# SyncE issues the chunk of the 128-slot stream before the chunk of the 64-slot stream in a two-layer hybrid mixer with experts

## The chip, the cores and the metric

The kernel is one program on one NeuronCore of a Trainium2 chip. TensorE (PE) multiplies, VectorE (DVE) and ScalarE (ACT) work elementwise, GpSimd (POOL) sets up constants, SyncE (SP) issues the transfers. They run side by side and meet through semaphores. Sixteen DMA engines bring weights from HBM into SBUF. The metric is the device time of one launch in microseconds, median of the runs; lower is better.

## The reference

Two layers work on 256 latent tokens and 256 context tokens of width 1024. Each layer is a modulated RMSNorm, an input projection, a mixer of three head groups, an output projection, then a second norm and a channel mixer. The channel mixer of the second layer is the part that matters here: eight SwiGLU experts of hidden width 2816, of which each token takes the best two.

```python
def swiglu(h, w1, w3, w2):
    return (jax.nn.silu(h @ w1) * (h @ w3)) @ w2

def moe_swiglu(h, w_r, b_r, w1, w3, w2):
    logits = (h @ w_r).astype(jnp.float32) + b_r.astype(jnp.float32)
    top_v, top_i = lax.top_k(logits, TOP_K)
    probs = jax.nn.softmax(top_v, axis=-1)
    combine = jnp.einsum('blk,blke->ble', probs, jax.nn.one_hot(top_i, N_EXPERTS, dtype=jnp.float32))
    out = jnp.zeros_like(h)
    for e in range(N_EXPERTS):
        out = out + combine[..., e, None].astype(h.dtype) * swiglu(h, w1[e], w3[e], w2[e])
    return out
```

All weights are float32. The three matrices of one expert are 34.6 MB, so the stage reads 277 MB.

## The kernel before

The first half of the program holds both mixers and the dense channel mixer of layer 0. The expert stage starts at about 820 us of the profiled span and ends at about 1582. It alone is touched.

Tokens are gathered into slots by expert. The experts are ordered by load. The four fuller ones form the t stream, with 128 slots each; the four emptier ones form the s stream, with 64 slots each. The fullest expert has 32 more slots, the x stream, which uses the t stream's weights in the first pass. A pass (`pair` on SyncE, `expert` on the other engines) works on one t expert and one s expert together; there are four passes.

The weights of an expert are cut into 33 chunks of 1 MiB (`PER_EXPERT`): 22 of w1 and w3 (`UP`), 11 of w2. Most are 128x2x1024, rows of 4 KB; chunks 16, 17, 19, 20 are 128x4x512 and chunks 18 and 21 are 128x8x256. In step j of a pass TensorE does the following:

- the t matmuls of chunk j (L1218 on), in three products of a high and a low part. ScalarE writes the high part `w_hi` from `raw` (L1589), VectorE the low part `w_lo` (L2187). There are three buffers for each part, so the split of chunk j+3 waits for TensorE's t matmuls of chunk j and for the landing of chunk j+3;
- the s matmuls of chunk j (`s_mm`), in full float32 and straight from the landed tile. They wait for the landing alone and end with an increment of `s_pe`;
- in the first pass, the x matmuls of chunk j+3, also straight from the t stream's landed tile.

Landed tiles: `raw` has five slots. Slots 0 to 2 are the ring of the t stream; slots 3 and 4 and the tile `raw_x` are the ring of the s stream. So every third s chunk goes through `raw_x`, which makes it easy to follow in the trace.

All these transfers are issued by SyncE, in program order, on one queue. SyncE itself waits until a slot is free. A slot of the t stream is free once VectorE has written `w_lo` from it (function `taken`, a wait on `dve_done`) and, in the first pass, once the x matmuls have used it. A slot of the s stream is free after the s matmuls (wait on `s_pe`). In step j of `pair` the s chunk that is issued is j+3 (`RING`), the t chunk is j+6 (`RING + AHEAD`). The first pass is written out, the second and third run in a hardware loop, the fourth is written out with `last=True` and stops issuing when there is nothing left to fetch.

Of the kernel before, what the change touches and what calls it, by code (L numbers as in the profile page):

```python
# [64 lines left out]
PER_EXPERT = UP + DOWN  # L65
# [9 lines left out]
RING = 3  # L75
# [126 lines left out]
def program(nc, a, out, known, marks):  # L202
    def at(*name):

        return known[name] if known else 1

    ctx = ExitStack()
    with ctx:
        def sem(name):
            return ctx.enter_context(nc.semaphore(name))  # L210
# [160 lines left out]
        s_dve, s_act, s_pe = sem("s_dve"), sem("s_act"), sem("s_pe")  # L371
# [97 lines left out]
        def s_raw(j):  # L469
            return raw_x[:, :] if j % RING == RING - 1 else raw[:, RING + j % RING, :]  # L470
# [21 lines left out]
        def _(sp):  # L492
# [42 lines left out]
            def expert_chunk(e, j, slot, landed):  # L535

                if j < UP:
                    m, k0, nk, c0, nc_ = UPC[j]
                    src = a[("moe_w1", "moe_w3")[m]][0].rearrange("e (k p) c -> (e k) p c", p=P)
                    src = src[bass.ds(e * KD + k0, nk), :, c0:c0 + nc_]  # L540
                    sp.dma_start(slot.rearrange("p (k c) -> p k c", k=nk), src.rearrange("k p c -> p k c"))\
                      .then_inc(landed[E_SLOT[j]], 16)
                else:
                    src = a["moe_w2"][0].rearrange("e (k p) c -> (e k) p c", p=P)
                    src = src[bass.ds(e * KF + 2 * (j - UP), 2), :, :]
                    sp.dma_start(slot.rearrange("p (k c) -> p k c", k=2), src.rearrange("k p c -> p k c"))\
                      .then_inc(landed[E_SLOT[j]], 16)

            K = at("per_expert", "dve")
            last = {E_SLOT[j]: j for j in range(PER_EXPERT)}  # L550

            def taken(j, shift):
                if j < PER_EXPERT:
                    sp.wait_ge(dve_done, (at("first_lo", j) if shift is None else at("e_lo", j) + shift) if j >= SPL or
                               shift is None else at("next_lo", j) - K + shift)
                else:
                    sp.wait_ge(dve_done, at("next_lo", j - PER_EXPERT) + shift)

            def t_chunk(e, j):
                expert_chunk(e, j, raw[:, E_SLOT[j], :], exp_in)  # L560

            def s_chunk(e, j):
                expert_chunk(e, j, s_raw(j), s_in)

            def pair(e, e_s, after, after_s, n, top=False, last=False):
                for j in range(PER_EXPERT):
                    if not last or j + RING < PER_EXPERT:
                        sp.wait_ge(s_pe, at("s_mm", j) + n * Ks)
                        s_chunk(e_s if j + RING < PER_EXPERT else after_s, (j + RING) % PER_EXPERT)
                    t = j + RING + AHEAD  # L570
                    if not last or t < PER_EXPERT + RING:
                        taken(j + AHEAD, n * K)
                        if top and j + AHEAD < PER_EXPERT:
                            sp.wait_ge(x_pe, at("x_mm", j + AHEAD))
                        t_chunk(e if t < PER_EXPERT else after, t % PER_EXPERT)

            def expert_of(turn):
                return sp.value_load(order_i[0:1, bass.ds(turn, 1)], min_val=0, max_val=NE - 1)
# [11 lines left out]
            Ks = at("per_s", "pe")  # L590
# [4 lines left out]
            e_s = expert_of(NE)  # L595
            for j in range(RING):
                s_chunk(e_s, j)
            for j in range(AHEAD):
                taken(j, None)
                sp.wait_ge(x_pe, at("x_mm", j))  # L600
                t_chunk(e, j + RING)
            pair(e, e_s, expert_of(1), expert_of(NE + 1), 0, top=True)
            with sp.Fori(1, NT - 1, 1) as n:
                pair(expert_of(n), expert_of(n + NE), expert_of(n + 1), expert_of(n + NE + 1), n)
            sp.wait_ge(x_dve, at("again"))
            pair(expert_of(NT - 1), expert_of(TURNS - 1), expert_of(NT), None, NT - 1, last=True)

            with sp.Fori(0, MORE, 1) as r:
# [116 lines left out]
        def _(pe):  # L725
# [10 lines left out]
            def tables(n):  # L736

                _, rows, _ = TABLES[n]
                return nc.tensor.transpose(STAT[:, P * n:P * n + rows], rows_sb[0:rows, n, :], ident[0:rows, 0:rows])
# [92 lines left out]
            def first_products(l):  # L832

                pe.wait_ge(dve_done, at("h_lo", l, 1, 0))
                take(("w_in", l, WIN_ORDER[0]))
                for k in range(KD):
                    pe.wait_ge(dve_done, at("h_lo", l, 1, k))
                    product(l, 0, 0, k)
                    if l == 1 and k == 0:
                        take(("w_in", l, WIN_ORDER[1]))  # L840
                    if l == 0 and k == 1:
                        product(l, 0, 1, k)
                        take(("w_in", l, WIN_ORDER[1]))
                        product(l, 1, 0, 0)
                        product(l, 1, 0, 1)
                    elif l == 1 or k > 1:
                        product(l, 1, 0, k)
                        product(l, 0, 1, k)
                    else:
                        product(l, 0, 1, k)  # L850
                    if l == 1:
                        product(l, 1, 1, k)
                if l == 0:
                    pe.wait_ge(table_in, 16 * sum(len(parts) for parts, _, _ in TABLES[1:]))
                    pe.wait_ge(dve_done, at("t", 0, 1, KD - 1))
                    for m in range(1, len(TABLES)):
                        i = tables(m)
                    i.then_inc(pe_done, pe_n("tables"))
                    for k in range(KD):
                        product(l, 1, 1, k)  # L860
# [244 lines left out]
            def turn_bank_free(j, de, ae, sd, sa, top, s):  # L1105

                users = [(SEL_AT, "sel", 0)] + [(at_, "t", p) for p, at_ in TURN_AT.items()]
                users += [(S_SEL_AT, "s_sel", 0)] * s + [(at_, "s", g) for g, at_ in S_TURN_AT.items() if s]
                users += [(X_SEL_AT, "x_sel", 0)] * top + [(at_, "x", n) for n, at_ in X_TURN_AT.items() if top]
                assert len({u[0] for u in users}) == len(users)  # L1110
                _, kind, n = max(u for u in users if u[0] < j)
                if kind == "sel":
                    pe.wait_ge(act_done, at("e_selT") + ae)
                    pe.wait_ge(dve_done, at("e_slot_w") + de)
                elif kind == "t":
                    pe.wait_ge(dve_done, at("e_hd", n) + de)
                elif kind == "s_sel":
                    pe.wait_ge(s_dve, at("s_selT") + sd)
                elif kind == "s":
                    pe.wait_ge(s_act, at("s_hd", n) + sa)  # L1120
                elif kind == "x_sel":
                    pe.wait_ge(x_dve, at("x_selT"))
                else:
                    pe.wait_ge(x_act, at("x_hd", n))
# [1323 lines left out]
```

## Time and profile before

| | |
|---|---|
| median of 3 runs | 1620.76 us (1618.61 to 1623.23) |
| profiled execution | 1618.61 us |
| its span | 1616.8 us |
| mean granted TensorE clock | 0.968 |
| busy PE / DVE / ACT | 1508.7 / 845.7 / 622.7 us |
| read from HBM | 395.55 MB |
| transfers of expert weights | 223 to `raw`, 44 to `raw_x`, 1 MiB each, median 8.4 and 8.3 us from issue to landing |

The profile is one execution of the program. The span runs from its first instruction to its last; the execution's time is 1.8 us longer. Of the other runs it differs by what one run differs from the next. "Busy" is time in which an engine executes; SyncE isn't counted, since it only issues and waits. In the rows below L541 and L546 are SyncE's issues of w1 or w3 and of w2 chunks, L727 is the helper through which every matmul goes, and the names before and behind the arrow are the written and the read tiles. s matmuls read `raw` or `raw_x` with `hcs` (gathered tokens) in the w1 and w3 part and with `xT` (where the hidden activations stand by then) in the w2 part; x matmuls read `raw` with `hcx`. An "idle before" in brackets names what ended it.

### The profile page before, as it was taken

How to read it: one execution, taken by the hardware profiler on the slowest of the kernel's cores; microseconds unless marked ns; L12 is line 12 of the kernel's file. 1: busy time of each engine (PE TensorE's matmuls, PEld its weight loads, DVE VectorE, ACT ScalarE, POOL GpSimd, SP SyncE). 2: the span in 40 equal slices, each digit the busy share in tenths (PEclk: the TensorE clock that was granted, in tenths of full speed). 3: DMA queues.
4: the chain of work that ended last, by engine and by line, in shares of the span. 5: the costliest groups of instructions: out<-in, count | busy, mean ns of one | idle time of the engine just before them, and what ended most of it. 6: DMA issues, size and time to landing. Idle time of an engine off the chain costs nothing.

```text
span 1616.8 us, 22394 instructions
## 1 busy us (share of the span) xinstructions
PE 1508.7 (93%) x8914; PEld 1063.4 (66%) x8915; DVE 845.7 (52%) x1115; ACT 622.7 (39%) x679; POOL 17.4 (1%) x56
## 2 busy tenths in 40 slices
PE   5999798999999998976879999999999999999995
PEld 3786485888888876953745575665766566655763
DVE  2898845333333234897564544445554555355544
ACT  2426723222123223457253433434443444344441
POOL 2000000000000001000000000000000000000000
PEclk9999899999999999997989999999999999999996
DMA  9632943822442233436269999889999999999990
GB/s 335 204 104 85 337 127 140 212 72 72 131 119 73 72 114 105 157 104 243 72 263 355 344 325 353 306 326 399 389 409 377 396 382 408 386 350 396 393 388 28
DMA packets 208664, 398.10 MB, mean 246 GB/s; under 512 B 12060, under 2 KB 123056, under 8 KB 208560
## 3 DMA queue, kind: packets, MB, share of 16 engines
q1 hardware_dynamic: 207968, 396.42, 68.4%
q8 instruction: 76, 1.25, 0.3%
q10 hardware_dynamic: 592, 0.21, 0.1%
q14 instruction: 28, 0.23, 0.0%
HBM read 395.55 MB, written 1.05 MB: 245 GB/s over the span
## 4 chain that ended last, share of the span: by engine, by line
PE 83%; DVE 6%; ACT 5%; DMA 3%; issue 3%; DVEq 0%; SPq 0%; ACTq 0%
PE bank L727 81%; DMA raw<-in_w_mod 2%; DVE xc L1986 1%; PE bank L1201 1%; DVE y L1884 1%; DVE tb L1756 1%; DVE h_lo L1764 1%; ACT la L1476 1%; DMA raw<-in_moe_w 1%; ACT w_hi L1355 0%; ACT li L1472 0%; ACT lr L1470 0%; ACT w_hi L1589 0%; ACT lm L1481 0%; DVE w_lo L1739 0%
## 5 line engine op out<-in xcount | busy, mean ns | idle before, releaser
L2187 DVE TENSOR_TENSOR w_lo<-raw,w_hi 128x2048 fp32r<-128x2048 f32 x135 | 309.3, 2292 | 268.4 <-ACT w_hi L1589 261.0
L1589 ACT ACTIVATE w_hi<-raw 128x2048 fp32r<-128x2048 f32 x135 | 258.2, 1913 | 429.0 <-PE bank L727 318.0
L727 PE MATMUL bank<-h_hi,w_hi 128*128 128x512 f32 (+1 forms) x768 | 285.7, 372 | 18.7 <-DVE h_lo L1764 16.3
L727 PE MATMUL bank<-h_lo,w_hi 128*128 128x512 f32 (+1 forms) x768 | 283.0, 369 | 0.0
L727 PE MATMUL bank<-h_hi,w_lo 128*128 128x512 f32 (+1 forms) x768 | 282.8, 368 | 0.0
L1355 ACT ACTIVATE w_hi<-raw 128x2048 fp32r<-128x2048 f32 (+1 forms) x64 | 113.7, 1776 | 214.6 <-PE bank L727 196.7
L727 PEld LDWEIGHTS bank<-h_hi,w_hi 128*128 128x128 f32 x768 | 147.1, 192 | 46.5 <-DVE h_lo L1764 19.8
L1739 DVE TENSOR_TENSOR w_lo<-raw,w_hi 128x2048 fp32r<-128x2048 f32 (+1 forms) x64 | 135.9, 2123 | 51.2 <-ACT w_hi L1355 51.0
L727 PEld LDWEIGHTS bank<-h_hi,w_lo 128*128 128x128 f32 x768 | 146.9, 191 | 23.5
L727 PEld LDWEIGHTS bank<-h_lo,w_hi 128*128 128x128 f32 x768 | 147.1, 191 | 23.0
L727 PE MATMUL bank<-w_hi,hc_hi 128*128 128x512 f32 (+1 forms) x384 | 153.8, 400 | 1.9 <-ACT w_hi L1589 1.9
L727 PE MATMUL bank<-w_lo,hc_hi 128*128 128x512 f32 (+1 forms) x384 | 144.6, 376 | 0.0
L727 PE MATMUL bank<-w_hi,hc_lo 128*128 128x512 f32 (+1 forms) x384 | 143.8, 374 | 0.0
L727 PE MATMUL bank<-raw,hcs 128*64 128x512 f32 (+2 forms) x736 | 116.5, 452 | 0.0
L727 PEld LDWEIGHTS bank<-w_hi,hc_hi 128*128 128x128 f32 x384 | 72.6, 189 | 47.0 <-issue 23.9
L727 PEld LDWEIGHTS bank<-w_hi,hc_lo 128*128 128x128 f32 x384 | 72.7, 189 | 14.3
L727 PEld LDWEIGHTS bank<-w_lo,hc_hi 128*128 128x128 f32 x384 | 72.9, 190 | 10.4
L2090 DVE TENSOR_TENSOR sq<-tb,bank 128x512 f32<-128x512 f32 x22 | 15.1, 688 | 121.0 <-ACT tb L1555 121.0
L727 PEld LDWEIGHTS bank<-raw,hcs 128*64 128x64 f32 x736 | 43.6, 136 | 48.1 <-issue 42.5
L727 PE MATMUL bank<-w_hi,hd_hi 128*128 128x512 f32 x176 | 73.0, 415 | 0.0
L1555 ACT ACTIVATE tb<-bank 128x512 f32<-128x512 f32 x22 | 13.2, 598 | 153.6 <-PE bank L727 153.6
L727 PE MATMUL bank<-f_hi,w_hi 128*128 128x512 f32 x176 | 69.1, 393 | 0.0
(299 smaller groups left out, 1862.7 us busy)
## 6 DMA issues: line engine op xcount, KB each, us to landing
raw<-in_moe_w SPq DMA_DIRECT2D x223, 1024.0 KB, 8.4
raw<-in_w_mod SPq DMA_DIRECT2D x48, 1024.0 KB, 7.8
raw_x<-in_moe_w SPq DMA_DIRECT2D x44, 1024.0 KB, 8.3
raw<-in_ffn_w SPq DMA_DIRECT2D x44, 512.0 KB, 5.4
raw<-in_w_in SPq DMA_DIRECT2D x18, 1024.0 KB, 5.3
raw<-in_ffn_w SPq DMA_DIRECT2D x16, 704.0 KB, 4.7
raw<-in_w_out SPq DMA_DIRECT2D x8, 1024.0 KB, 5.5
x_in<-in_ctx SPq DMA_DIRECT2D x1, 1024.0 KB, 4.9
```

Of the source, the lines that this page charges most:

```text
L727: return nc.tensor.matmul(dst, lhsT, rhs, start=first, stop=last)
L1201: i = nc.tensor.transpose(bank[TURN_BANK][:, P * t:P * t + P], hid[:, p % 2, P * t:P * t + P], ident[:, :])
L1355: nc.scalar.activation(w_hi[:, s % SPL, 0:n], raw[:, POS[c] % RAW, 0:n], ACT.Copy)\
L1476: nc.scalar.activation(la[:, t, :], lr[:, t, :], ACT.Exp, scale=cln[:, k:k + 1], bias=cln[:, k:k + 1]).then_inc(act_done, act_n())
L1589: nc.scalar.activation(w_hi[:, j % SPL, :], raw[:, E_SLOT[j], :], ACT.Copy)\
L1739: V.tensor_tensor(w_lo[:, s % SPL, 0:n], raw[:, POS[SPLIT[s]] % RAW, 0:n], w_hi[:, s % SPL, 0:n].bitcast(F32), ALU.subtract).then_inc(dve_ ...
L1756: i = V.scalar_tensor_tensor(tb[:, d % 2, tok(s)], xT[:, d, tok(s)], amp[:, l, w - 1, d, s:s + 1], STAT[:, tok(s)], ALU.mult, ALU.mult)
L1764: i = V.scalar_tensor_tensor(h_lo[:, d, tok(s)], tb[:, d % 2, tok(s)], shift, h_hi[:, d, tok(s)].bitcast(F32), ALU.add, ALU.subtract)
L1884: i = V.scalar_tensor_tensor(out_v, in_v, w, out_v, ALU.mult, ALU.add)
L1986: i = V.scalar_tensor_tensor(out_v, cxp[:, t, :, k:k + 256], w, out_v, ALU.mult, ALU.add)
L2090: V.tensor_tensor(sq[:, i11 % 2, :], tb[:, i11 % 2, :], bank[2 * (s0 % 3) + 1][:, :], ALU.mult)\
L2187: V.tensor_tensor(w_lo[:, j % SPL, :], raw[:, E_SLOT[j], :], w_hi[:, j % SPL, :].bitcast(F32), ALU.subtract).then_inc(dve_done, dve_n(name ...
```

## The change

In each step of `pair` the two blocks are exchanged. Before, SyncE waited for the s matmuls of step j and issued the s chunk, then waited for the split and issued the t chunk. Now the t chunk's waits and issue come first. The transfers, their sizes, their slots and the conditions of each are the same; only SyncE's order differs. The order of the instructions on the four other engines is unchanged.

```diff
             def pair(e, e_s, after, after_s, n, top=False, last=False):
                 for j in range(PER_EXPERT):
-                    if not last or j + RING < PER_EXPERT:
-                        sp.wait_ge(s_pe, at("s_mm", j) + n * Ks)
-                        s_chunk(e_s if j + RING < PER_EXPERT else after_s, (j + RING) % PER_EXPERT)
                     t = j + RING + AHEAD
                     if not last or t < PER_EXPERT + RING:
                         taken(j + AHEAD, n * K)
                         if top and j + AHEAD < PER_EXPERT:
                             sp.wait_ge(x_pe, at("x_mm", j + AHEAD))
                         t_chunk(e if t < PER_EXPERT else after, t % PER_EXPERT)
+                    if not last or j + RING < PER_EXPERT:
+                        sp.wait_ge(s_pe, at("s_mm", j) + n * Ks)
+                        s_chunk(e_s if j + RING < PER_EXPERT else after_s, (j + RING) % PER_EXPERT)
```

SyncE at the start of the hardware loop over the second and third pass, steps 0 to 2, before. An ISA row with a wait is a wait that stands by itself; s_pe counts the s matmuls, dve_done VectorE's instructions.

```order
L568 ISA
L541 ISA [waits s_pe]
L541 DMA raw_64<-in_moe_w1 128x2x1024
L554 ISA
L541 ISA [waits dve_done]
L541 DMA raw_64<-in_moe_w3 128x2x1024
L568 REGISTER_ALU
L541 ISA [waits s_pe]
L541 DMA raw_64<-in_moe_w3 128x2x1024
L554 REGISTER_ALU
L541 ISA [waits dve_done]
L541 DMA raw_64<-in_moe_w3 128x2x1024
```

The same place in the changed kernel.

```order
L554 ISA
L541 ISA [waits dve_done]
L541 DMA raw_64<-in_moe_w3 128x2x1024
L574 ISA
L541 ISA [waits s_pe]
L541 DMA raw_64<-in_moe_w1 128x2x1024
L554 REGISTER_ALU
L541 ISA [waits dve_done]
L541 DMA raw_64<-in_moe_w3 128x2x1024
L574 REGISTER_ALU
L541 ISA [waits s_pe]
L541 DMA raw_64<-in_moe_w3 128x2x1024
```

The s chunk 3 (w1, behind the wait on s_pe) stood in front of the t chunk 6 (w3, behind the wait on dve_done); now it stands behind it, and so in each step.

The same exchange further on in the loop, where the t stream fetches chunks 16 and 17 (128x4x512) and the s stream chunks 13 and 14, before.

```order
L554 REGISTER_ALU
L541 ISA [waits dve_done]
L541 DMA raw_64<-in_moe_w1 128x4x512
L568 REGISTER_ALU
L541 DMA raw_x_68<-in_moe_w3 128x2x1024 [waits s_pe]
L554 REGISTER_ALU
L541 ISA [waits dve_done]
L541 DMA raw_64<-in_moe_w1 128x4x512
```

And in the changed kernel.

```order
L541 ISA [waits dve_done]
L541 DMA raw_64<-in_moe_w1 128x4x512
L574 REGISTER_ALU
L541 DMA raw_64<-in_moe_w3 128x2x1024 [waits s_pe]
L554 REGISTER_ALU
L541 ISA [waits dve_done]
L541 DMA raw_64<-in_moe_w1 128x4x512
L574 REGISTER_ALU
L541 DMA raw_x_68<-in_moe_w3 128x2x1024 [waits s_pe]
```

Between the two t chunks there stood the s chunk for `raw_x` (chunk 14); now chunk 13 stands there and the chunk for `raw_x` comes behind the second t chunk.

## Rows read from the trace of the kernel before

**Rows 1.** The page: busy time of each engine over the span.

```profile
PE 1508.7 (93%) x8914; PEld 1063.4 (66%) x8915; DVE 845.7 (52%) x1115; ACT 622.7 (39%) x679; POOL 17.4 (1%) x56
```

**Rows 2.** Busy time by stretch, one expert pass (us, busy and count, clock, DMA share, GB/s).

```profile
1212.00:1390.00 178.00, 177.79 (x915) 111.49 (x915) 93.58 (x73) 75.46 (x61) 0.00 (x0) 1.00 1.02 393
```

**Rows 3.** Waits, 1028 to 1582 us (who for whom: us in total, times, longest).

```profile
ACT w_hi L1589 <- DMA raw<-in_moe_w: 104.0, 35, 4.1
PEld bank L727 <- DMA raw_x<-in_moe_w: 1.4, 4, 0.4
```

**Rows 4.** Instructions in order of time near 1239 us (start, length, engine, operation).

```profile
1236.97 1.94 PE L727 MATMUL bank<-raw,hcs 128*64 128x512 f32 x8
...
1239.09 0.37 SPq L541 DMA_DIRECT2D raw<-in_moe_w  x1
...
1239.10 2.29 DVE L2187 TENSOR_TENSOR w_lo<-raw,w_hi 128x2048 fp32r<-128x2048 f32 x1 [1.06 <-ACT w_hi L1589]
...
1241.57 0.37 SPq L541 DMA_DIRECT2D raw<-in_moe_w  x1
```

**Rows 5.** The tile raw, the one transfer issued at 1241.57 us.

```profile
DMA to landing us min/median/max: 5.1/5.1/5.1
```

**Rows 6.** DMA throughput in 40 slices, 1228 to 1268 us, then 1268 to 1388 us.

```profile
GB/s 414 385 426 377 262 311 410 418 422 410 98 0 119 373 414 393 422 414 418 410 422 422 401 406 426 410 401 401 418 410 401 393 414 356 414 381 307 406 365 258
...
GB/s 391 397 416 408 414 411 408 397 396 395 402 356 380 391 384 377 350 357 400 395 402 363 396 411 407 411 410 410 408 406 412 407 411 408 412 407 408 408 407 411
```

**Rows 7.** Busy tenths of the DMA engines in 40 slices, 1048 to 1088 us.

```profile
DMA  8999699993000007899999999999989999999999
```

**Rows 8.** ScalarE and weight loads near 1347 us; the tile raw_x, 1330 to 1350 us.

```profile
1344.42 1.92 ACT L1589 ACTIVATE w_hi<-raw 128x2048 fp32r<-128x2048 f32 x1 [3.25 <-DMA raw<-in_moe_w]
1349.55 1.92 ACT L1589 ACTIVATE w_hi<-raw 128x2048 fp32r<-128x2048 f32 x1 [2.72 <-DMA raw<-in_moe_w]
...
1347.30 0.20 PEld L727 LDWEIGHTS bank<-raw_x,xT 128*64 128x64 f32 x4 [0.36 <-DMA raw_x<-in_moe_w]
...
L546 SPq DMA_DIRECT2D raw_x<-in_moe_w x2: 372/372/373, 1334.4 to 1349.5; - x2
DMA to landing us min/median/max: 12.5/12.6/12.8
```

**Rows 9.** The tile raw_x and the matmuls that use the transfer, one pass earlier, one later.

```profile
L546 SPq DMA_DIRECT2D raw_x<-in_moe_w x1: 372/372/372, 1172.6 to 1172.6; - x1
DMA to landing us min/median/max: 12.5/12.5/12.5
...
1185.57 0.65 PE L727 MATMUL bank<-raw_x,xT 128*64 128x512 f32 x2
...
L546 SPq DMA_DIRECT2D raw_x<-in_moe_w x1: 372/372/372, 1515.0 to 1515.0; - x1
DMA to landing us min/median/max: 12.6/12.6/12.6
...
1527.86 0.65 PE L727 MATMUL bank<-raw_x,xT 128*64 128x512 f32 x2
```

**Rows 10.** The t stream near 1345 us: the split of a chunk, and its first matmul.

```profile
1341.21 2.29 DVE L2187 TENSOR_TENSOR w_lo<-raw,w_hi 128x2048 fp32r<-128x2048 f32 x1 [2.27 <-ACT w_hi L1589]
...
1349.59 0.48 PE L727 MATMUL bank<-w_hi,hd_hi 128*128 128x512 f32 x1
```

**Rows 11.** The tile raw_x in the first pass, 860 to 1030 us.

```profile
DMA to landing us min/median/max: 4.8/5.0/8.3
```

**Rows 12.** TensorE's short idle in the first pass; busy time and clock there and after 1403.

```profile
898.24 1.07 PE L727 MATMUL bank<-raw,hcx 128*32 128x256 f32 x16 [0.58 <-ACT gsx L1606]
...
890.00:900.00 10.00, 9.42 (x70) 5.06 (x67) 6.23 (x8) 3.83 (x4) 0.00 (x0) 1.00 0.93 330
...
1402.84 0.49 PE L727 MATMUL bank<-w_hi,hc_hi 128*128 128x512 f32 x1 [1.86 <-ACT w_hi L1589]
...
1403.00:1407.00 4.00, 4.00 (x11) 3.13 (x12) 1.67 (x2) 0.00 (x0) 0.00 (x0) 0.57 1.01 387
```

## The prediction

> **What bounds the kernel now.** I read the page's busy line first: TensorE is busy 93% of the span, more than any other engine [rows 1]. The change touches only SyncE's issue order in the expert stage, so I then read the stretches by expert pass. In the third pass TensorE is busy 177.79 of 178 us at clock 1.00, while the DMA engines are busy too (share 1.02, 393 GB/s) [rows 2]. Both are full at once, so what counts is who waits for whom. Over the last three passes ScalarE waits for weights 35 times, 104.0 us in all, but the array's weight loads wait for a landing in raw_x only 4 times, 1.4 us together [rows 3], and those short waits lie under matmuls that still run. TensorE sets the time, and transfers arrive just before they are needed.
>
> The two streams of weights have very different reserves. I read them at chosen chunks, as landing against first use.
>
> The s stream (64 slots, matmuls straight from the landed tile): the chunk issued at 1334.4 lands 12.5 us later, at 1346.9, and its first weight load starts at 1347.30, released by that landing [rows 8]. Reserve 0.4 us. One pass earlier: 1172.6 + 12.5 = 1185.1 against 1185.57, reserve 0.5. One pass later: 1515.0 + 12.6 = 1527.6 against 1527.86, reserve 0.3 [rows 9].
>
> The t stream (128 slots, split by ScalarE and VectorE first): the chunk whose split ends on VectorE at 1341.21 + 2.29 = 1343.50 meets its first matmul at 1349.59 [rows 10]. Reserve 6.1 us.
>
> **How the transfers run.** A t chunk lands at 1344.42 (ScalarE starts on it at once) and the next at 1349.55; an s chunk lands between them, at 1346.9 [rows 8]. They alternate as SyncE's list does, one chunk per 5.13 / 2 = 2.56 us, or 1.049 MB / 2.56 us = 409 GB/s, which the slices show (407 to 412) [rows 6]. With 12.5 us from issue to landing, four to five chunks stand ahead of a new one. So in this stretch the moment of issue matters little, the place in the row decides. By the Trainium skill, "DMA: Bandwidth & Descriptors", section Queues, rings and completion order, completion is not in order per issuing engine: a later transfer may finish first. The rows above show landings in order of issue; if the rule held here, the first rival's sum (+6.2 us) would apply.
>
> The row is not always full. After each change of pass the transfers catch up and the engines run dry: 98, 0 and 119 GB/s in the three slices from 1238 to 1241 [rows 6], zeros near 1060, one pass earlier [rows 7]. From 1241 to 1388 no slice is empty. Whatever the new order loses at the dry spot stays lost for the rest of the pass.
>
> **The change, part by part.** It removes and adds no instruction. In each of the 33 steps of a pass, SyncE now first waits for VectorE's split of t chunk j+3 and issues t chunk j+6, and only then looks at TensorE's s matmuls of step j and issues s chunk j+3.
>
> 1. The wait in front of the s chunk. At the dry spot the s matmuls of the step run 1236.97 to 1238.91, and the s chunk is issued at 1239.09. The split ends at 1239.10 + 2.29 = 1241.39, and the t chunk is issued at 1241.57 [rows 4]. In the new order the s chunk can't go before that: 1241.57 - 1239.09 = 2.48 us later.
> 2. The chunk ahead of it. The t chunk now finds the row empty; the s chunk starts when it is through, 2.56 us on. Together 2.48 + 2.56 = 5.04 us later than before.
> 3. The t chunk gains nothing. It starts at 1241.57 in either order: it was behind an s chunk that started at 1239.09 and was through at 1241.65, and it lands 5.1 us after issue [rows 5]. Its reserve was 6.1 us anyway, so an earlier landing shortens only ScalarE's wait, which nobody waits for. That excludes a gain from this side.
> 4. From there the row is full, t and s alternate, and every s chunk lands about 5.04 us later against an unmoved TensorE. Where the reserve was 0.4 us, TensorE must be late by 5.04 - 0.4. Nothing pays it back: TensorE is busy 99.9% of the pass [rows 2], so its delay goes to the end.
> 5. The waits queued behind. SyncE does nothing else in this stage. The t chunk behind a late s chunk has its 6 us of reserve plus TensorE's own delay. ScalarE and VectorE keep their order.
> 6. The first pass: s chunks take 4.8 to 8.3 us there [rows 11]. From issue to use are at least the 12.9 us of the later pass (1334.4 to 1347.3) plus three blocks of a third stream's matmuls, 1.07 us each [rows 12], 16.1 us. The reserve is 7.8 us or more, over 5.04. No cost. It is the same at each change of pass, where the transfers have caught up. So three passes pay.
>
> Sum: 3 x 5.04 - (0.5 + 0.4 + 0.3) = 13.9 us. The profiled execution took 1618.61 us (span 1616.8), so 1632.5 in its terms. The median of the runs shown is 1620.76, 2.15 us above it, which gives 1634.7. I forecast 1634.5 us.
>
> Bounds of the shift per pass, since no row shows SyncE in the new order: at least 2.48 us (the wait alone counts), 3 x 2.48 - 1.2 = +6.2 us; at most a whole split in front of the s chunk, 1.92 us on ScalarE [rows 8] and 2.29 us on VectorE [rows 10], if TensorE's s matmuls are through before it begins: 4.21 + 2.56 = 6.77 us per pass, 3 x 6.77 - 1.2 = +19.1. I take 5.04, since the rows of the dry spot are the place where it is decided.
>
> A chunk's price could be seen otherwise. The same page of the Trainium skill, section Bandwidth (Where 436 GB/s comes from), says that HBM binds at about 358 GB/s for one core. A chunk would then take 1.049 / 358 = 2.93 us, and the sum would be 1.1 us higher. The slices here hold 407 to 412 GB/s, so the measurement decides against it.
>
> **Rivals.**
>
> *Only one of the two terms counts.* If landings were not strictly in order of issue, or the row had slack later, the shift would be the wait alone: +6.2 us, 1626.9 by the median. For it: the order is read from few chunks. Against it: no empty slice after 1241, and steady 2.56 us steps.
>
> *The waits also lower the clock.* TensorE will now stand still often for some tenths of a us. After an idle of 1.86 us before 1402.84 the clock was 0.57 of full over 1403 to 1407 [rows 12], which costs 4 x 0.43 = 1.7 us. Against it: idle of 0.58 us at 897.7 stands beside a clock of 1.00 from 890 to 900 [rows 12]. One such fall per pass gives 13.9 + 5.1 = +19.0, 1639.8; two give 1644.9.
>
> *Not slower.* The reserve at the tight point is what is left after a long catch-up race. From 1246.67 (1241.57 + 5.1) to 1344.42 there are 36 chunks, 2.71 us each, not 2.56: slices of 350 to 391 GB/s from 1301 to 1325 [rows 6], where the chunks come in smaller pieces. If the new order let all run at 2.56 us, 36 x 0.15 = 5.5 us per pass would come back, more than the loss. It decides once 3 of these 5.5 us come back: +13.9 - 9.0 = +4.9, which is 0.3%; with all of it 13.9 - 16.5, 1618 or so. Against it: pieces and sizes are unchanged. I give it an even result of about 1624.
>
> **How the numbers follow.** Forecast 0.62 (its own range 1631 to 1638), one term only 0.16, clock 0.14, not slower 0.08. The range 1626 to 1641 leaves out most of the last and about half of the clock's cases. A difference under 0.3% (4.9 us) can't be told from none with this kernel. Slower by over 0.3%: 0.62 + 0.14 and three quarters of 0.16, 0.88. Within: 0.04 from the one-term case and 0.06, 0.10. Faster: 0.02.
>
> **What the new profile would show.**
> - SyncE's issues in pairs, t chunk first, s chunk within about 0.5 us behind it. If the s chunk comes 2 us later still, step 1 is too small.
> - Slices of the DMA engines as full as before from the dry spot on. If there are new empty slices, step 4 is wrong upwards.
> - TensorE idle before matmuls on raw and raw_x, released by their landing: some 14 us in all, from about step 13 to 26 of the last three passes, none over 1 us, none in the first pass. If it is near 6 us, the one-term case holds; if near zero, the mechanism is wrong.
> - The raw_x flight in the tight stretch shorter, 10.5 to 11 us, not 12.5: issued with the t chunk, yet landing three steps of 5.13 us after the one before.
> - ScalarE's 104.0 us of waiting for landings falls under 20 us, because TensorE becomes the later of its two conditions.
> - Clock 1.00 in the passes but for one stretch near 1405.
>
> The forecast is wrong if s chunks keep landing where they did, or if the clock falls at the new waits.

## The result, and the profile after

The changed kernel takes 1634.73 us (median of 5 runs, 1630.55 to 1637.11); the kernel before takes 1620.76 (median of 5 on the same chip, 1616.17 to 1623.74). The ratio is 1.0085, 95% interval 1.0059 to 1.0110: slower by 14.0 us, where 13.9 was worked out and 1634.5 forecast. The profiled execution took 1638.21 us (span 1636.5), somewhat above the median.

The page of the changed kernel, busy time first and then the chain of waits:

```profile
PE 1514.5 (93%) x8914; PEld 1068.2 (65%) x8915; DVE 846.9 (52%) x1115; ACT 622.5 (38%) x679; POOL 17.4 (1%) x56
...
PE 70%; DMA 11%; DVE 9%; ACT 6%; issue 3%; SPq 1%; DVEq 0%; ACTq 0%
PE bank L727 68%; DMA raw<-in_moe_w 5%; DMA raw_x<-in_moe_w 4%; DVE w_lo L2187 2%; ACT w_hi L1589 2%; DMA raw<-in_w_mod 2%; DVE y L1884 1%; DVE xc L1986 1%; DVE tb L1756 1%; ACT la L1476 1%; DVE w_lo L1739 1%; DVE h_lo L1764 1%; DVE lr L2033 1%; ACT li L1472 0%; ACT lr L1470 0%
```

Every engine does the same instructions as in [rows 1]. What is new stands in the chain: transfers of expert weights into raw and raw_x hold 9% of it. Before, the chain was 83% TensorE and 3% DMA.

The four expert passes of the changed kernel as stretches, columns as in [rows 2]:

```profile
836.80:1045.20 208.40, 205.81 (x1473) 124.84 (x1465) 93.64 (x107) 75.04 (x66) 0.00 (x0) 0.99 0.91 331
1045.20:1232.50 187.30, 182.41 (x925) 115.22 (x921) 93.07 (x73) 75.31 (x62) 0.00 (x0) 0.99 0.97 370
1232.50:1417.40 184.90, 179.68 (x909) 112.26 (x905) 93.52 (x74) 75.82 (x62) 0.00 (x0) 0.99 0.99 376
1417.40:1601.20 183.80, 179.14 (x907) 112.09 (x905) 93.06 (x73) 75.38 (x62) 0.00 (x0) 0.99 0.95 365
```

The same four passes of the kernel before:

```profile
836.80:1043.20 206.40, 204.15 (x1469) 123.59 (x1461) 93.13 (x107) 75.07 (x66) 0.00 (x0) 1.00 0.93 338
1043.20:1223.50 180.30, 180.30 (x923) 113.63 (x921) 92.84 (x73) 75.37 (x62) 0.00 (x0) 1.00 1.00 382
1223.50:1402.50 179.00, 177.27 (x907) 110.56 (x905) 93.61 (x75) 77.39 (x63) 0.00 (x0) 1.00 1.02 392
1402.50:1581.60 179.10, 178.46 (x905) 111.71 (x905) 92.02 (x72) 73.89 (x61) 0.00 (x0) 0.99 0.96 368
```

Length less busy time is TensorE's idle time. In the last three passes it is 4.89 + 5.22 + 4.66 = 14.8 us after, and 0 + 1.73 + 0.64 = 2.4 us before. With 0.3 us in the first pass (2.59 against 2.25) that makes 12.7 of the 19.6 us between the two sums. The rest is busy time: 5.2 us in the last three passes and 1.7 in the first, most of it clock (four falls against one, below). The DMA share falls only because the same transfers now stand in a longer time.

The waits of the changed kernel, 1028 to 1600 us, which answer to [rows 3]:

```profile
ACT w_hi L1589 <- PE bank L727: 329.4, 98, 11.7
...
PEld bank L727 <- DMA raw<-in_moe_w: 16.5, 25, 1.6
...
PE bank L727 <- DMA raw<-in_moe_w: 11.4, 17, 1.4
...
PEld bank L727 <- DMA raw_x<-in_moe_w: 10.0, 18, 1.2
...
PE bank L727 <- DMA raw_x<-in_moe_w: 2.1, 4, 0.8
```

The matmuls themselves now wait for a landing 21 times, 13.5 us together, where [rows 3] had only weight loads that waited for it. ScalarE's 104.0 us of waiting for landings are gone: TensorE is always the later of its two conditions.

The dry spot of the same pass as in [rows 4], in order of time:

```profile
1246.02 1.94 PE L727 MATMUL bank<-raw,hcs 128*64 128x512 f32 x8
...
1248.15 2.29 DVE L2187 TENSOR_TENSOR w_lo<-raw,w_hi 128x2048 fp32r<-128x2048 f32 x1 [1.06 <-ACT w_hi L1589]
...
1250.62 1.00 SPq L541 DMA_DIRECT2D raw<-in_moe_w  x2
...
1251.24 0.37 SPq L541 DMA_DIRECT2D raw<-in_moe_w  x1
```

The s matmuls are through at 1247.96, the split at 1250.44, and SyncE then issues two chunks in a row, at 1250.62 and 1251.24 (the first issue row holds both, the last one is the second of them by itself). The s chunk goes 1251.24 - 1247.96 = 3.28 us after its matmuls, where it was 0.18 us before. The tile raw, the transfers issued at 1250.62 (t) and at 1251.24 (s), which answer to [rows 5]:

```profile
DMA to landing us min/median/max: 5.5/5.5/5.5
...
DMA to landing us min/median/max: 7.4/7.4/7.4
```

The t chunk finds the row empty; the s chunk lands at 1258.6, 2.5 us behind it. DMA throughput in 40 slices, 1232 to 1272 us, which answers to [rows 6]:

```profile
GB/s 168 422 422 418 426 238 205 385 434 414 406 377 410 381 401 426 258 49 4 66 188 401 422 422 414 389 369 418 401 401 340 319 393 385 410 389 307 426 426 389
```

Here and below, "the row" is the line of chunks that are issued and not yet landed. It runs dry at 1248 and is back by about 1252.5 (the slice of 1252 is 46% full), 19.6 us after the pass's first t matmul at 1232.9. In [rows 6] it is back by about 1240.7 (119 of 410 GB/s in that slice), 16.9 us after that pass's first t matmul at 1223.8: 2.7 us earlier. After it no slice is empty, as before.

Two of the new waits, in the same pass (TensorE in order of time):

```profile
1335.02 1.20 PE L727 MATMUL bank<-raw,hcs 128*64 128x128 f32 x18 [1.00 <-DMA raw<-in_moe_w]
...
1351.98 0.44 PE L727 MATMUL bank<-raw,hcs 128*64 128x128 f32 x4 [1.36 <-DMA raw<-in_moe_w]
```

And the tile raw_x between them, issued at 1350.8, against 12.5 us in [rows 8]:

```profile
L546 SPq DMA_DIRECT2D raw_x<-in_moe_w x1: 373/373/373, 1350.8 to 1350.8; - x1
...
DMA to landing us min/median/max: 11.3/11.3/11.3
```

### The profile page after: what moved, and what is told of

It reads as the page before. It is cut to its first block, busy times and chain, and to the rows that moved or that the text cites. A ratio compares the mean times of both kernels' runs of the same rounds, so it can differ in the third digit from the quotient of the medians.

```text
span 1636.5 us, 22394 instructions
## 1 busy us (share of the span) xinstructions
PE 1514.5 (93%) x8914; PEld 1068.2 (65%) x8915; DVE 846.9 (52%) x1115; ACT 622.5 (38%) x679; POOL 17.4 (1%) x56
## 4 chain that ended last, share of the span: by engine, by line
PE 70%; DMA 11%; DVE 9%; ACT 6%; issue 3%; SPq 1%; DVEq 0%; ACTq 0%
PE bank L727 68%; DMA raw<-in_moe_w 5%; DMA raw_x<-in_moe_w 4%; DVE w_lo L2187 2%; ACT w_hi L1589 2%; DMA raw<-in_w_mod 2%; DVE y L1884 1%; DVE xc L1986 1%; DVE tb L1756 1%; ACT la L1476 1%; DVE w_lo L1739 1%; DVE h_lo L1764 1%; DVE lr L2033 1%; ACT li L1472 0%; ACT lr L1470 0%
## 5 line engine op out<-in xcount | busy, mean ns | idle before, releaser
L727 PEld LDWEIGHTS bank<-h_hi,w_lo 128*128 128x128 f32 x768 | 146.2, 190 | 23.7
L727 PE MATMUL bank<-raw,hcs 128*64 128x512 f32 (+2 forms) x736 | 116.5, 452 | 10.7 <-DMA raw<-in_moe_w 10.5
L2090 DVE TENSOR_TENSOR sq<-tb,bank 128x512 f32<-128x512 f32 x22 | 15.1, 688 | 121.4 <-ACT tb L1555 121.4
L727 PE MATMUL bank<-w_lo,hd_hi 128*128 128x512 f32 x176 | 71.2, 404 | 0.0
```

Source lines behind the costliest of these rows:

```text
L727: return nc.tensor.matmul(dst, lhsT, rhs, start=first, stop=last)
L2090: V.tensor_tensor(sq[:, i11 % 2, :], tb[:, i11 % 2, :], bank[2 * (s0 % 3) + 1][:, :], ALU.mult)\
```

## The experiments

All times are medians, and each ratio is against the kernel before on the same chip (1621.82 for the first four, 1621.54 for the next four, 1622.24 for the last two). "Waits for landings" are the rows PE bank <- DMA of the expert passes, as above. "Shift" is how much later an s chunk lands against the first t matmul of its pass than in the first profile of the kernel before. Every run on record has a mean granted clock; a span times (1 less that clock) is an estimate of what the lower clock cost it, about 53 us in the kernel before, nearly all of it outside the expert passes. The code cuts are shortened.

**The new order in the first pass alone.** Theory: the first pass has reserve and pays nothing.

```
for give in (give_t, give_s) if top else (give_s, give_t):   # each the old lines
    give()
```

> The new order in the first pass only; the other three passes as before. Theory (an s chunk lands 2.48 + 2.56 us later, and only passes whose reserve falls to 0.3 to 0.5 us pay): the first pass has 7.8 us of reserve or more, so TensorE waits for no s chunk and the time is that of before, within 0.3%; no idle of TensorE released by a landing after 860 us. Rival (the swap costs wherever it stands, about a quarter of +14 us per pass): +3.5 us, and waits of TensorE in the first pass.

Measured: 1623.29 us, ratio 1.0007 (0.9984 to 1.0030). Waits of this kernel, 1028 to 1610 us:

```profile
PEld bank L731 <- DMA raw_x<-in_moe_w: 2.5, 7, 0.4
...
PE bank L731 <- DMA raw<-in_moe_w: 0.2, 1, 0.2
```

No cost, as expected: the one idle of 0.2 us lies in the fourth pass, which has the old order. The first pass is safe in either order.

**The new order in steps 0 to 9 of each pass alone.** The dry spot lies in them.

```
for give in (give_t, give_s) if j < 10 else (give_s, give_t):
    give()
```

> The new order in steps 0 to 9 of every pass, the order of before from step 10 on. This keeps the loss at the dry spot and gives the s chunk its place in the row back before the tight stretch. Theory: s chunks land 2.48 us late in the tight stretch, TensorE idles 3 x 2.48 - 1.2 = 6.2 us by landings, time +6 us. Rival A (the dry spot does not matter, the order in the tight stretch does): idle 0, time as before. Rival B (everything is lost at the dry spot): idle near 14 us, as in the changed kernel.

Measured: 1634.16 us, ratio 1.0062 (1.0038 to 1.0086). TensorE's waits for landings in this kernel:

```profile
PE bank L731 <- DMA raw<-in_moe_w: 3.3, 6, 0.8
...
PE bank L731 <- DMA raw_x<-in_moe_w: 0.2, 1, 0.2
```

The shift of s chunk 12 is about 5 us (72.1 against 66.7 us after the start of the second pass); at chunk 13, the first with s first again, it falls by 2.5 to 2.6 us in each pass, and 2 to 3 us stay (4.2 late in the second pass). So the place in the row comes back when the order is turned back, and the part lost at the dry spot does not.

The sizes were missed: 3.5 us of waits for landings where 6.2 were expected, and 12.3 us of time (by the ratio 10.1) where 6 were. A good part of the excess is clock. In the profile the five stretches of half clock cost about 11.5 us, against 1.7 in the kernel before, and TensorE's idle in the last three passes is 9.9 us against 2.4; together 17 of the 18.9 us between the two spans. Over the runs on record the mean clock is 0.9648 in nine of this kernel and 0.9673 in 26 of the kernel before: by the estimate above about 4 us more, which leaves some 7 of the 11.6 us between the mean spans. Why the clock is lower here stays open.

**The new order from step 10 on alone.** The theory of the prediction expects the place alone, 2.56 us per pass.

```
for give in (give_t, give_s) if j >= 10 else (give_s, give_t):
    give()
```

> The other half: the order of before in steps 0 to 9 of every pass, the new order from step 10 on. Theory: only the chunk in front counts, 2.56 us and at most 0.4 us more where the row isn't quite full at step 10: TensorE idles 3 x 2.56 - 1.2 = 6.5 us up to 7.7 us by landings, time +7 us. Rival A: near 14 us, as in the changed kernel. Rival B: idle near 0, time as before.

Measured: 1631.18 us, ratio 1.0054 (1.0033 to 1.0075). Waits of this kernel, 1028 to 1610 us:

```profile
PE bank L731 <- DMA raw<-in_moe_w: 8.1, 13, 1.4
PE bank L731 <- DMA raw_x<-in_moe_w: 4.3, 3, 2.0
```

The expectation was missed: 12.4 us of idle, well over the 6.5 to 7.7. The kernel's transfers where the order changes, 1285 to 1305 us in 40 slices:

```profile
GB/s 410 410 410 426 401 410 393 418 410 410 410 410 418 410 393 352 205 139 123 307 365 418 373 393 430 418 418 401 361 250 332 385 377 406 397 410 414 422 403 315
```

The kernel before over the same time (its pass began 5.6 us earlier):

```profile
GB/s 393 426 410 401 410 401 401 426 410 418 385 389 393 389 393 393 393 401 393 401 401 418 373 393 389 397 393 410 410 406 416 377 369 360 354 350 348 354 373 383
```

The row was not full: it falls to 123 GB/s at 1294. In the steps around it a chunk's flight is 8.0 to 8.7 us, 3.0 to 3.7 over the 5.0 of a chunk alone, so a little over one chunk (2.56 us) stands ahead. An issue that comes 3 us later uses that up, and the landings pause. At s chunk 13, the first behind the turn, the shift jumps by 3.1 to 3.6 us: the place, and 0.5 to 1.0 of pause. By s chunk 18 it is near 5 us again (5.1, 5.6 and 3.8 in the three passes). So "unfilled time" adds to "place in the row" where the row is shallow, not at the dry spot only.

That does not explain all of the 5 us. In the third and fourth pass s chunk 17 lands 4.2 us behind the chunk in front of it, where the kernel before has 2.7 (in the third pass it is issued at 1313.0 and flies 12.2 us, the chunk in front 1312.4 and 8.6), and TensorE's longest idle of this kernel, 1.9 and 2.0 us, is the wait for it. The row is deep there and no slice from 1316 to 1332 is under 335 GB/s. What holds this chunk back stays open.

**The new order from step 20 on.** If the row's depth decides, there it is over two chunks (flights of 11.4 to 12.0 us in the third pass) and must hide the later issue, leaving the place alone.

```
for give in (give_t, give_s) if j >= 20 else (give_s, give_t):
    give()
```

> The order of before in steps 0 to 19 of every pass, the new order from step 20 on. With the swap from step 10 on TensorE had waited for s landings nearly as long as in the changed kernel (about 15 us, not the 6.5 to 7.7 that I had expected), and the first t chunk after the swap landed 6.2 us after its issue: the row was little over one chunk deep there, so an s chunk that comes 3 us late leaves a pause. Theory now: the shift is the place (2.56 us) plus what the later issue leaves unfilled, and at step 20 an s chunk takes 10.8 to 11.7 us to land in the kernel before, over two chunks stand ahead, so nothing stays unfilled: shift 2.56 us, waits for s landings 3 x 2.56 - 1.2 = 6.5 us. Rival (a swap costs two chunks' time wherever it stands, whatever the depth): 13 us or more.

Measured: 1628.23 us, ratio 1.0041 (1.0026 to 1.0056). Transfers at the turn, 1328 to 1348 us, and the waits of this kernel:

```profile
GB/s 387 406 393 393 410 422 406 385 389 393 385 397 393 414 397 414 401 375 387 391 334 342 354 383 391 385 410 393 401 410 393 426 418 410 418 401 401 410 393 434
...
PEld bank L731 <- DMA raw_x<-in_moe_w: 8.1, 5, 2.7
PE bank L731 <- DMA raw_x<-in_moe_w: 5.8, 3, 2.2
```

No hole. The landings after the turn stay 2.5 to 2.7 us apart, and the s chunks are late by one place, once per pass: from s chunk 22 to 23 the shift jumps by 2.5 to 2.6 us, and the longest wait at the weight loads is 2.7. TensorE's idle is 5.8 us where 6.5 were expected, the time 6.0 us more than before. So the place by itself is shown, with its size; the other term is what the dry spot and the turn at step 10 add to it.

**Is it the row at all, or SyncE's order and its waits?** The changed order, but each t chunk loads only its first 0.5 MiB. Half of the t weights are not loaded, so part of the computation is left out.

```
 sp.dma_start(raw[:, E_SLOT[j], 0:CW // 2]..., src[first half])   # 0.5 MiB, same waits, new order
```

> The changed order, but each t chunk loads only its first half, 0.5 MiB (the second half of the slot keeps old values, so that part of the computation is changed). A pair then takes 3.8 us of transfer and not 5.1, and TensorE needs about 5 us for a step. Theory: the row is never full, the s reserve never shrinks below about 3 us, TensorE does not wait although SyncE has exactly the order and the waits of the changed kernel: time as before, 1616 to 1624 us. Rival (SyncE's added wait costs by itself): still +6 us or more over before.

Measured: 1621.02 us, ratio 0.9995 (0.9977 to 1.0012). Of waits for landings, this one row is left:

```profile
PEld bank L736 <- DMA raw_x<-in_moe_w: 0.4, 1, 0.4
```

That is the weight loads; no matmul waits for a landing. The same instructions, waits and order cost nothing once the row has room. What costs is the full row. Two things lie under the equal time: the mean clock was lower (0.9646 against 0.9677, about 5 us by the estimate), and none of the idles that the kernel before has in its last three passes (2.4 us) is left in the list of waits. No run has the light row in the old order, so the argument rests on the waits more than on the time.

**The t chunk in two halves, the s chunk between them; and both halves behind it as a control.** The s chunk then has half a chunk ahead of it.

```
t_half(..., 0)      # waits for the split, as t_chunk did; 0.5 MiB
s_chunk(...)        # waits for the s matmuls
t_half(..., 1)      # the control: s_chunk first, then both halves
```

> Each t chunk is fetched in two transfers of 0.5 MiB; SyncE waits for the split, issues the first half, then the s chunk, then the second half. Same wait in front of the s chunk as in the changed kernel, half the bytes. Theory: shift 2.48 + 1.28 = 3.76 us, TensorE idles 3 x 3.76 - 1.2 = 10.1 us by landings, time +10 us over the next kernel (halves in the order of before). Rival (the wait alone counts): 6.2 us. Rival (the order of issue alone counts, whatever the size in front): 14 us as in the changed kernel.

> Control for the one before: t chunks in two transfers of 0.5 MiB, both behind the s chunk, the order of before. Theory: time as before within 0.3% if a transfer of 0.5 MiB costs half of one of 1 MiB in the full row; else every pair takes longer and TensorE idles at the tight point.

Measured: 1630.17 us, ratio 1.0055 (1.0033 to 1.0077) with the half in front, 1623.26, ratio 1.0009 (0.9995 to 1.0022) for the control. Waits with the half in front:

```profile
PE bank L743 <- DMA raw<-in_moe_w: 7.3, 12, 0.8
...
PE bank L743 <- DMA raw_x<-in_moe_w: 1.2, 3, 0.4
```

The waits are 8.5 us against 13.5 and 12.0 in the two profiles of the changed kernel, so half the place gives back about a third of the idle; the ratio lies below theirs, with intervals that overlap. Expected were 10.1 us of idle and 10 us over the control; the idle is 1.6 us less, the time 6.9 us over the control. Both lie between the wait alone (6.2) and the whole chunk (14), nearer to the wait. The control's matmuls wait 0.5 us in two waits together: the halves themselves cost nothing that can be told.

**Is the t stream's reserve 6.1 us?** The order of before, each t chunk issued one step later.

```
LAG = 2                               # AHEAD = 3 stays for the ring
t = j + RING + LAG
taken(j + LAG, None if top and j + LAG < SPL else n * K)
```

> The order of before (s chunk first), but the t stream is fetched one chunk less far ahead: in step j SyncE issues t chunk j+5, not j+6. Theory (t chunks have 6.1 us of reserve that nobody uses, and what decides for s is where it stands from the dry spot on, which stays): time as before within 0.3%; the s reserve at the tight point stays 0.3 to 0.5 us; the t reserve falls by a pair of chunks, 5.1 us, to about 1 us, or a few waits of TensorE for a split, 2 us in all at most. Rival (how much stands in the row when an s chunk is issued decides): one chunk fewer in front, s reserve 2.9 us.

Measured: 1643.62 us, ratio 1.0130 (1.0100 to 1.0161), slower than the changed kernel itself. The expectation was missed. Waits of this kernel, and one of the five at L1202 with the busy time and clock around it:

```profile
ACT w_hi L1590 <- DMA raw<-in_moe_w: 233.3, 75, 4.5
...
PEld bank L1202 <- DVE hd_lo L2287: 18.9, 9, 4.6
...
PE bank L1202 <- DVE hd_lo L2287: 12.4, 5, 4.2
...
1530.02 0.47 PE L1202 MATMUL bank<-ident,hid 128*128 128x128 f32 x1 [4.15 <-DVE hd_lo L2287]
...
1528.00:1535.00 7.00, 4.98 (x14) 4.09 (x15) 4.25 (x3) 2.58 (x4) 0.00 (x0) 0.52 1.06 387
```

No matmul waits for a landing after 860 us. But ScalarE stands at w_hi for a late chunk, VectorE behind it at w_lo, and behind that in VectorE's list stands hd_lo, the split of the hidden activations, for which TensorE's transposes at L1202 wait. Before, the same wait at L1201 was 0.5 us. A reserve read from a chunk's own first matmul misses what is queued behind its split. The chain of queues is read from these rows; I did not test it by itself. Half clock comes on top: beside each of the three long waits (3.7, 3.4 and 4.2 us, in front of 1159.4, 1341.5 and 1530.0) stands such a stretch. Over its six runs the mean clock is 0.9623, against 0.9673 before, by the estimate about 9 of the 21.9 us between the mean spans.

**The changed kernel and the kernel before, each profiled again.**

> The changed kernel once more, for a second profile. In its first profile TensorE idled 13.6 us by landings (7 + 9 + 7 places in the last three passes), and the rest of the 19.7 us between the two spans was clock: half speed for 3.4 us at the end of each of the four passes, against one such fall in the kernel before. Theory: the idle repeats within 1.5 us, since it follows from the places in the row; the number of clock falls does not, it is chance from run to run, and the medians differ by the idle alone, 14 us. Rival: four falls again, so the falls belong to the new order.

> The kernel before once more, for a second profile: how far its waits, its clock falls and its span repeat. Theory: no idle of TensorE by landings over 1 us in all, span within 5 us of 1616.8, the number of clock falls at the changes of pass different from the one of the first profile.

Measured: the changed kernel 1636.01 us, ratio 1.0079 (1.0059 to 1.0099), span 1633.8; the kernel before 1620.59 in one run, span 1618.9. Waits of the changed kernel, second profile:

```profile
PEld bank L727 <- DMA raw<-in_moe_w: 15.9, 24, 1.4
PE bank L727 <- DMA raw<-in_moe_w: 10.4, 17, 1.1
PEld bank L727 <- DMA raw_x<-in_moe_w: 9.3, 18, 0.9
```

The landing waits repeat (10.4 us, and 1.6 in raw_x, against 13.5), so they are the kernel's. The kernel before shows none again. The stretches of half clock repeat in part: near 1222 and 1590 both profiles of the changed kernel have one, near 1034 and 1406 the first alone; the kernel before has one at 1403 in its first profile, two at 1033 and 1392 in its second.

## Why the prediction was right, step by step

The mechanism holds in the main. That 13.9 and 14.0 agree to 0.1 us is luck: the interval of the ratio alone runs from 9.6 to 17.8 us, and terms that the sum left out cancel.

1. *The wait in front of the s chunk, 2.48 us.* Right: 1250.44 - 1247.96 = 2.48 us again. The s chunk leaves another 0.6 us later, the time SyncE takes to issue the t chunk first. That 0.6 lies under the t chunk's own transfer.
2. *The t chunk ahead, 2.56 us.* Right. The s chunk lands 2.5 us behind the t chunk. The shift of a landing against the pass's start is 5.1 and 5.6 us at step 4 of the second and third pass (23.7 to 28.8, 20.2 to 25.8); in the fourth, 25.2 against 21.9, and 20.3 in the profile with only the first pass changed, so 3.3 to 4.9. At s chunk 18, where the waits are, it is 6.0, 5.9 and 3.1: not three times the same, as the sum has it, but 15.0 in all against 15.1.
3. *The t chunk gains nothing, its reserve of 6.1 us is waited for by nobody.* This step is half wrong. The run with the later t chunks showed that the reserve does not protect TensorE: as its rows read, hd_lo stands behind the split. It did no harm here, because the changed order makes no t chunk later. And there is a small gain that step 3 excluded (the boundary, below).
4. *From the dry spot the row is full; each s chunk lands 5.04 us late, less 0.4 of reserve.* Right in result: 13.5 and 12.0 us of visible idle. Mis-stated in mechanism. The row is only a little over one chunk deep until about step 12, and turning the order there makes a hole of its own. With the new order from the start it makes no difference; I take it that the pause is taken once, at the first dry spot.
5. *No cost behind.* Right: no new row of waits for another engine, and the light row costs nothing.
6. *The first pass pays nothing.* Right: 1.0007 with it changed alone, and its idle is 2.6 us against 2.25 before.

What the sum left out cancels. At the boundary between the third and fourth pass, with the old order late in the pass, TensorE stands idle; with the new order it hardly does. TensorE in the kernel before, second profile:

```profile
1405.87 0.49 PE L727 MATMUL bank<-w_hi,hc_hi 128*128 128x512 f32 x1 [2.38 <-ACT warm L1647]
```

The changed kernel at the same place:

```profile
1417.79 0.49 PE L727 MATMUL bank<-w_hi,hc_hi 128*128 128x512 f32 x1 [0.36 <-issue]
```

In the twelve profiles, the six that end the pass s first have 1.9 to 2.7 us there (1.86 in [rows 12]), the one with the half in front 0.64, and the five that end it t first 0.36 at most. The name of the releaser differs ([rows 12] has w_hi), and w_hi was ready earlier: ScalarE had ended it at 1404.80 in the second profile, 1.07 us before the matmul. Why the new order spares it was only looked at, not tested: it stays open. It gives back about 2 us. About as much, 2.6 us, is taken by busy time at full clock and by idles too short for the list of waits. I put that down to weight loads that wait for a landing under a running matmul; it is not shown.

The clock. Four stretches of the changed kernel's first profile, the granted clock being the third figure from the right:

```profile
1034.00:1038.00 4.00, 4.00 (x14) 3.34 (x14) 0.00 (x0) 0.00 (x0) 0.00 (x0) 0.58 0.99 338
1221.00:1225.00 4.00, 4.00 (x16) 3.32 (x16) 0.00 (x0) 0.00 (x0) 0.00 (x0) 0.59 1.02 407
1405.00:1409.00 4.00, 4.00 (x18) 3.44 (x18) 0.19 (x1) 0.00 (x0) 0.00 (x0) 0.63 1.03 412
1590.00:1594.00 4.00, 4.00 (x13) 3.15 (x13) 0.00 (x0) 0.00 (x0) 0.00 (x0) 0.57 0.32 126
```

Over most of each stretch the clock is at the lower of its two levels (1.2 of 2.4 GHz), with TensorE busy all the time; one costs 4 x 0.41 = 1.6 us. All four stand about 11 us before a change of pass, and none at the landing waits of 1335 or 1352. The kernel before had one in its first profile and two in its second; the second profile of the changed kernel had two. So the 19.7 us between the two first spans are about 13.5 of visible landing waits and 5 of clock (three more falls), less 1.5 at the boundary, and the 2.6 just named. For the medians the granted clock of all runs tells more: 0.9668 in twelve executions of the changed kernel, 0.9674 in 58 of the kernel before, by the estimate 1.4 us, hardly more than the scatter of such means. So the 14.0 us are waits, with little clock or none.

The rivals. *One term only* (+6.2): ruled out by the shift of 5.1 and more, and by the runs that change the order from step 10 and from step 20, which show the terms apart. Its premise, landings out of order, does not hold here. By the Trainium skill, "DMA: Bandwidth & Descriptors", section Queues, rings and completion order, a later transfer may finish first. In this queue of equal chunks the t chunk issued 0.6 us ahead lands 2.5 us ahead, and in the ten profiles in which a t chunk is one transfer, all 267 chunks land in the order of their issue. *The waits lower the clock*: not in the changed kernel, where no fall stands at a landing wait; the longest of them is 1.4 us. Beside longer idles some do stand. In the kernel turned at step 20, one landing wait of 2.25 us has half clock beside it:

```profile
1536.32 1.12 PE L731 MATMUL bank<-raw_x,xT 128*64 128x512 f32 x2 [2.25 <-DMA raw_x<-in_moe_w]
...
1536.00:1540.00 4.00, 3.68 (x11) 1.05 (x12) 3.06 (x9) 0.10 (x1) 0.00 (x0) 0.57 1.03 411
```

Its two others, 1.9 and 1.7 us, have none. In the profile with only the first pass changed, 2.69 us of idle at the boundary, up to 1405.18, stand beside a clock of 1.00 over 1403 to 1410. Over the twelve profiles, of eleven idles of 1.7 to 2.7 us in the expert passes four have a fall beside them, and so have all three of 3.4 to 4.2 us. So for longer waits the rival stays open.

*Not slower*: the slices did not fill up.

Of the signs listed, four came as written: issues in pairs, no new empty slices, ScalarE's wait gone, and some 14 us of idle in the last three passes with nearly nothing new in the first. Three were off: the longest waits are 1.0 to 1.4 us and not under 1; the flights in raw_x are 10.7 to 12.3 us in the tight stretch of the third pass and not 10.5 to 11; and the clock fell four times, not once.

No version beats the kernel before: none of the runs points to a gain, and TensorE is busy in its last three passes to within 2.4 us already.

## What to carry to other kernels

When two streams share one queue, price a change of order as two terms: the place in the row (one chunk's transfer time) and the time the row runs empty because the issue comes later. The second is hidden if the row is well deeper than the delay; read that from flight less the flight of a chunk alone. Give the earlier place to the stream with the smaller reserve, and take a reserve from everything that stands behind the waiting instruction, not from the chunk's own first use.

## What the runs showed of the hardware

A queue of 1 MiB chunks lands strictly in order of issue here, 2.56 us apart when it is full (409 GB/s), 2.7 where the chunks come as 128x4x512 and 3.0 as 128x8x256, and 5.0 to 5.5 us from issue to landing when it is empty. Halving the t chunks left the time as it was (1.0009). In that control 29 of the 402 landings are recorded ahead of the transfer in front, by up to 0.55 us, each a t half behind an s chunk. The two halves count on one semaphore, so such a record can be early; whether they really overtook is not shown.

Falls of the clock, 1.6 us each, come and go between profiles of one and the same kernel (four and two in the expert stage), so the spans of single profiles differ by some 3 us for that alone, and one profile can't show what a change does to the clock; the mean granted clock over many runs can.
